# Attention units of a decoder kernel in another order, half adds placed before the next row maximum, samples moved forward, and output weights loaded and split inside the attention loop

## The reference

```python
conv_out = silu(layer_norm(depthwise_causal(a_ext, w_dw) + b_dw))
s = q @ k.T * 64 ** -0.5 + (c_q - c_k)          # c: running sums of log forget gates
att = softmax(where(pos_k <= pos_q, s, -inf)) @ v   # 8 heads of 64
mix = concat([conv_out, att]) @ w_out_even      # 1024 x 1024
```

## Time and profile before

| | us |
|---|---|
| median of 3 runs | 2755.68 (2751.33 to 2757.24) |
| profiled execution, its own time | 2756.72 |
| its span in the profile | 2755.1 |
| TensorE busy | 2581.8 (94%) |
| VectorE busy | 1357.0 (49%) |
| ScalarE busy | 711.6 (26%) |
| POOL busy | 427.2 (16%) |
| first row maximum of attention | at 327.54 |
| last row maximum | at 601.22 |
| first matmul of the output product | at 630.57 |

### The profile page before, as it was taken

The page is one execution under the profiler, slowest core; times in us unless marked ns, Lnnn a source line. Parts: engine busy times, 40 slices in busy tenths (PEclk is TensorE's granted clock), DMA queues, the critical chain, the costliest instruction groups (busy, mean ns, idle before and its releaser), DMA issues.

```text
span 2755.1 us, 38472 instructions
## 1 busy us (share of the span) xinstructions
PE 2581.8 (94%) x15545; PEld 2471.4 (90%) x15545; DVE 1357.0 (49%) x2034; ACT 711.6 (26%) x1218; POOL 427.2 (16%) x423
## 2 busy tenths in 40 slices
PE   7999588877899999999999999999999999999996
PEld 7999455557799999999999999988999999999995
DVE  4788755556753323333334644577433333333355
ACT  4110354444341111111111531225211111111114
POOL 3299233322200000000002200032000000000023
PEclk9999799998999999999999999999999999999998
DMA  7110412122011111111111221121111111111101
GB/s 230 50 31 0 137 57 70 54 86 93 25 52 47 40 38 47 47 46 47 44 34 47 60 91 46 38 101 38 47 47 47 41 37 46 46 39 40 45 16 65
DMA packets 169615, 152.55 MB, mean 55 GB/s; under 512 B 17057, under 2 KB 144337, under 8 KB 169432
## 3 DMA queue, kind: packets, MB, share of 16 engines
q1 hardware_dynamic: 161920, 133.92, 16.0%
q0 software_dynamic: 6208, 15.94, 1.8%
q10 hardware_dynamic: 1320, 0.24, 0.1%
HBM read 131.43 MB, written 18.93 MB: 55 GB/s over the span
## 4 chain that ended last, share of the span: by engine, by line
PE 87%; DVE 8%; issue 2%; ACT 2%; DMA 1%; SPq 0%; DVEq 0%; POOL 0%; ACTq 0%
PE PS L746 26%; PE PS L747 26%; PE PS L748 26%; PE PS L964 2%; DVE ST L1738 2%; PE PS L902 1%; DVE AL L1560 1%; PE PS L754 1%; PE PS L906 1%; PE PS L955 1%; DVE SPR L1666 1%; PE PS L919 1%; DVE RSD L1849 1%; PE PS L942 0%; PE PS L760 0%
## 5 line engine op out<-in xcount | busy, mean ns | idle before, releaser
L746 PE MATMUL PS<-AH,WHI 128*128 128x368 f32 x3360 | 1122.4, 334 | 43.6 <-DVE Y L1912 14.1
L747 PE MATMUL PS<-AL,WHI 128*128 128x368 f32 x3360 | 1114.8, 332 | 0.0
L748 PE MATMUL PS<-AH,WLO 128*128 128x368 f32 x3360 | 1111.3, 331 | 0.0
L746 PEld LDWEIGHTS PS<-AH,WHI 128*128 128x128 f32 x3360 | 635.3, 189 | 54.5 <-DVE Y L1912 18.2
L747 PEld LDWEIGHTS PS<-AL,WHI 128*128 128x128 f32 x3360 | 634.4, 189 | 2.8 <-issue 0.6
L748 PEld LDWEIGHTS PS<-AH,WLO 128*128 128x128 f32 x3360 | 634.7, 189 | 0.0
L1942 DVE TENSOR_TENSOR HF<-S,PS 128x368 f32<-128x368 f32 x132 | 70.9, 537 | 698.1 <-ACT S L1179 698.1
L746 PE MATMUL PS<-HH,WHI 128*128 128x368 f32 x1056 | 349.9, 331 | 3.2 <-DVE Y L1953 3.2
L747 PE MATMUL PS<-HL,WHI 128*128 128x368 f32 x1056 | 349.6, 331 | 0.0
L748 PE MATMUL PS<-HH,WLO 128*128 128x368 f32 x1056 | 349.3, 331 | 0.0
L1953 DVE TENSOR_TENSOR Y<-Y,PS 128x368 f32<-128x368 f32 x480 | 251.6, 536 | 154.9 <-PE PS L748 154.9
(11 more groups left out here) (267 smaller groups left out, 2250.9 us busy)
## 6 DMA issues: line engine op xcount, KB each, us to landing
RAW<-in_w_ffn_gate SPq DMA_DIRECT2D x44, 512.0 KB, 3.8
RAW<-in_w_ffn_up SPq DMA_DIRECT2D x44, 512.0 KB, 5.0
RAW<-in_w_ffn_down SPq DMA_DIRECT2D x44, 512.0 KB, 3.5
RAW<-in_w_in_even SPq DMA_DIRECT2D x20, 512.0 KB, 4.9
Y<-x_spill SPq DMA_DIRECT2D x16, 552.0 KB, 6.0
KR<-in_cache_k SPq DMA_DIRECT2D x32, 256.0 KB, 3.1
RAW<-in_w_in_odd SPq DMA_DIRECT2D x16, 512.0 KB, 4.5
x_spill<-Y POOLq DMA_DIRECT2D x3, 1472.0 KB, 6.5
```

What stands on the lines that cost most here:

```text
L746: pe.matmul(out, wh, xh, start=first, stop=False)
L747: pe.matmul(out, wh, xl, start=False, stop=False)
L748: return pe.matmul(out, wl, xh, start=False, stop=last)
```

## The change

The order in each head becomes 0, 7, 1, 6, 2, 5, 3 and then 4, 8 or 8, 4, with the sample fourth in odd heads (place 3). The key turns move: an even head h has those of its own sequence at places 1 to 4 and the first two of the next sequence at places 7 and 8; the odd head after it has the other two at places 0 and 1. The page loads, the samples' queries and new keys, and the turn back of a sample's result move with them. On VectorE the half add of n-6 comes before the maximum of n. At the end, output weight rows 0 and 1 are loaded as soon as the last sample's values are done; ScalarE splits them, and makes the first mixed rows, inside the last steps of its loop, and VectorE makes their low parts there. On TensorE the turn back of a sample's result waits for the centring (`la_cen`) instead of the copy of the variance, and the convolution's norm for one sample result more. One of the convolution's reciprocals moves from the loop's last steps to behind it.

```diff
-PAR8 = (1, 1, 0, 0, 1, 1, 0, 0)
-HEADS = tuple((0, 1, 2, 3, 4, 5) + ((None,) if h % 2 else ()) + ((6, 8, 7), (6, 7, 8))[PAR8[h]] for h in range(NH))
+HEADS = ((0, 7, 1, 6, 2, 5, 3, 4, 8),
+         (0, 7, 1, None, 6, 2, 5, 3, 4, 8),
+         (0, 7, 1, 6, 2, 5, 3, 8, 4),
+         (0, 7, 1, None, 6, 2, 5, 3, 8, 4),
...
         def key_turn(n):
-            return (h, r - 1) if h < NH and 1 <= r < 5 else None
+            if h == NH:
+                return None
+            if h % 2 == 0:
+                return (h, r - 1) if 1 <= r < 5 else (h + 1, r - 7) if 7 <= r < 9 else None
+            return (h, r + 2) if r < 2 else None
```

In SyncE's queue:

```diff
                 if k == 6:
-                    sp.wait_ge(qk_done, 1 + SMP[-1])
+                    sp.wait_ge(pv_done, 2 + SMP[-1])
+                    for n in (0, 1):
+                        load(2 * ST_OUT0 + n, (2 * ST_OUT0 + n) % 4, out_rows(0, n))
                     sp.wait_ge(sb_done, NS // 2)
                     sp.wait_ge(att_evac, 1 + NU)
-                    for n in range(4):
+                    for n in (2, 3):
                         load(2 * ST_OUT0 + n, (2 * ST_OUT0 + n) % 4, out_rows(0, n))
```

In POOL's loop:

```diff
-                if h % 2 and r == 3:
+                if h % 2 and r == 0:
                     new_keys(h // 2)
```

In ScalarE's loop and behind it:

```diff
+                if n in (NU + 1, NU + 2):
+                    act.wait_ge(pv_done, 2 + SMP[-1])
+                    split_centred(ST_OUT0, (n - NU - 1,))
+                if n == NU + 3:
+                    act.wait_ge(qk_done, NU)
+                    act.wait_ge(att_evac, 1 + FIRST[4])
+                    mix_high(2, QKV, (0, 1))
+                if n == NU + 4:
+                    act.wait_ge(sb_evac, NS // 2)
+                    mix_high(2, QKV, (2,))
...
-                if h % 2 and r == 2 and n < NU:
+                if h % 2 and r == 1 and n < NU:
                     queries(h // 2)
...
-            split_centred(ST_OUT0)
             act.wait_ge(att_evac, 1 + NU)
-            mix_high(2, QKV)
             mix_high(3, QKV)
             split_centred(ST_OUT0 + 1)
```

In VectorE's loop and behind it:

```diff
                     inverse(*UNITS[n - 1])
+                if n > LAG_V:
+                    gathered(*UNITS[n - LAG_V - 1])
                 if n < NU:
                     peak(*UNITS[n])
-                if n > LAG_V:
-                    gathered(*UNITS[n - LAG_V - 1])
...
-                if NU < n <= NU + 2:
-                    inverse_conv(n - NU - 1)
-            split_centred(ST_OUT0)
+                if n == NU + 1:
+                    inverse_conv(0)
+                if n in (NU + 2, NU + 3):
+                    split_centred(ST_OUT0, (n - NU - 2,))
+                if n == NU + 4:
+                    mix_low(2, (0, 1))
+            mix_low(2, (2,))
+            inverse_conv(1)
```

More of the change, by code:

```diff
@@ L374, in build @@
         BACK = {u + LAG_V + 3: p for p, u in enumerate(SMP)}
-        assert all(place(n)[1] == 4 or n >= NU for n in BACK)
+        assert all(place(n)[1] == 1 or n >= NU for n in BACK)
         def norm_step(n, h0, r0):
@@ L478, in _ @@
             for h in range(NH - 1):
[L479 to L482, removed]
+                if h % 2 == 0:
+                    key_pages(h + 1)
+                    if h:
+                        values(h + 1)
+                else:
+                    key_pages(h + 1)
                     values(h + 1)
+                    value_pages(h // 2 + 1)
             def residual(k):
@@ L971, in turn_back @@
                 pe.wait_ge(exp_done, WIDE[2 * p + 1] + 3)
-                if p < NC:
-                    pe.wait_ge(la_copy, p + 1)
+                pe.wait_ge(la_cen, 2 * min(p + 1, NC))
                 for c in range(HT):
@@ L980, in conv_norm @@
                 pe.wait_ge(exp_done, WIDE[h - 1] + 3)
-                pe.wait_ge(sb_evac, (h - 1) // 2)
+                pe.wait_ge(sb_evac, h // 2)
                 norm_product(ONES_H, YSA, s_in, s_res, c, 2)
@@ L1305, in _, with mix_high @@
             act.copy(CQ2[64:128, :], KBS[0:64, PAST:KS]).then_inc(cq_ready, 1)
+            def mix_high(q, src, cs=range(NC)):
+                for c in cs:
+                    act.copy(AH[:, 2 * q:2 * q + 2, chunk(c)], src[:, 2 * q % 4:2 * q % 4 + 2, chunk(c)]).then_inc(la_hi, 1)
             for n in range(NU + LAG_V + 1):
@@ L1336, in _ @@
                     head_high(h + 1, r - 3)
-            split_centred(ST_OUT0)
[L1339 to L1343, removed]
             act.wait_ge(att_evac, 1 + NU)
-            act.wait_ge(sb_evac, NS // 2)
-            mix_high(2, QKV)
             mix_high(3, QKV)
@@ L1793, in inverse_conv, with mix_low @@
                 dve.reciprocal(RSV[:, c, :], RSV[:, c, :]).then_inc(la_rs, 1)
+            def mix_low(q, cs=range(NC)):
+                for c in cs:
+                    src, qs = AEXT if q < 2 else QKV, slice(2 * q, 2 * q + 2)
+                    dve.wait_ge(la_hi, 3 * OUT_TILES[0].index(q) + c + 1)
+                    low(AL[:, qs, chunk(c)], src[:, 2 * q % 4:2 * q % 4 + 2, chunk(c)], AH[:, qs, chunk(c)]).then_inc(m_ready, 1)
             for n in range(NU + LAG_V + 1):
@@ L1815, in _ @@
                     head_low(h + 1, r - 5)
-                if NU < n <= NU + 2:
-                    inverse_conv(n - NU - 1)
-            split_centred(ST_OUT0)
[L1821 to L1826, removed]
+                if n == NU + 1:
[6 more added lines that the diff above has]
+            inverse_conv(1)
             def mix_low_even(o):
-                if o == 0:
-                    mix_low(2)
                 if o == 1:
```

## The result

The changed kernel takes 2771.01 us (median of 5 runs, 2767.24 to 2776.98) beside 2751.33 for the kernel before on the same chip: ratio 1.0066, 95% interval 1.0048 to 1.0084. (A ratio here is estimated from all runs together with its interval, so it differs a little from the quotient of two medians.) It is slower, by 16 us in the profiled execution (own time 2772.58 against 2756.72; span 2770.9 against 2755.1).

What follows compares the result with a forecast made beforehand. It took attention to be bound by VectorE and ScalarE handing each other work while TensorE waits. Loop +7.1, clock +4 and tail -15.25 gave -4.1 us: 2752.6, or 2752 as median, range 2736 to 2770.

Steps and rivals of the forecast that it cites:

- the walk: Attention loop stepped through in each engine's queue order at full clock: 280.8 us against 273.7 before, +7.1 us.
- the key turn's wait for the copy of bank 6: Sign in the attention loop: TensorE's key turns wait above 15 us for ScalarE's copy instead of 6.4, singly 2 to 4.
- the half adds' wait: Sign in the attention loop: TensorE's value products wait well under 35 us for VectorE's half add, 35.3 us before.
- the maximum waiting for ScalarE through the half add: Sign on VectorE: the row maximum no longer waits for scores alone but for ScalarE's half copy, by way of the half add.
- the loads before the last maximum: Sign at the loop's end: loads of the output weights are issued before the last row maximum.
- The tail: From last row maximum to output product: early output weights start the product 14.1 us after it instead of 29.35, -15.25 us.
- the clock term: Attention loop: TensorE's lost clock adds 4 us, half of 9 us, with slow matmuls hidden more often; ends 0 and +9.
- the sum: Whole kernel: +7.1 loop, +4 clock, -15.25 tail make -4.1 us, so 2752.6 us against the profiled execution's 2756.72.
- Rival 2: Attention loop: longer standing at key turns drops the clock at some 12 places, +22 us on the walk, 2770 us; chance 0.20.
- The half adds: VectorE's half add before the maximum: removes up to 35.3 us of TensorE's wait, but queues the maximum behind ScalarE's half copy.
- all 35.3 us go: Lower bound of the loop term: TensorE's whole wait for half adds vanishes and nothing replaces it, -31 us.
- The later steps: From the output product on: steps keep their distances from its start, so they add no time.

Runs made afterwards that it cites:

- kept-busy kernel: Changed kernel plus 8 needless matmuls of 512 columns before the key turns at 12 places: 2758.27 us, ratio 1.0021 to the kernel before.
- the two that free the key turn: Changed kernel with bank 6 copied before the exponential, 2737.38 us, ratio 0.995; changed kernel with key turns behind value products, 2751.63 us, ratio 0.9998.

## Why the prediction was wrong

**What held.** The rows of the walk came as said: the key turn's wait for the copy of bank 6 above 15 us (30.9 in 13, longest 3.3; 3.6 had been walked), the half adds' wait "well under 35" (11.3), the maximum waiting for ScalarE through the half add, the loads before the last maximum. The tail was predicted at 14.1 us and took 14.94.

**The step that failed is the clock term**, "I take half, +4, with 0 and +9 as ends". The walk at full clock gave 280.8 us, the loop took 301.39: 20.6 us beside a term of 4. These 16.6 us are most of the 20 us by which the profiled execution missed the sum; the tail is 0.8 and the later steps 2.5. By heads the excess over the walk is 2.0, 3.9, 2.4, 2.1, 1.5, 4.0, 2.4 and 2.3 us, largest in heads 1 and 5, whose clock is 0.83 and 0.85. The argument had been that slow matmuls would be "hidden more often" since TensorE waits more. It was the wrong way round: in these traces the clock falls in or just behind waits, and the slow matmuls come right behind, in front of the next scores (512.53 to 515.45 above) that all engines wait for. The clock lost is 0.14 x 301 = 42 us against 0.08 x 274 = 22 before. The amount was the fault: I had carried over the 15 us of before, though my walk had just found TensorE standing longer at places 3, 4 and 8.

How much of the 20.6 us is clock is shown only in part. The kept-busy kernel took 3.0 of the 4.0 us of excess from head 5 and 2.7 of 3.9 from head 1 by a higher clock, 6.0 over the loop. The rates at hand, 0.6 us for each us lost before and 2.9 for 3.5 between the two head 2, make 42 us of clock 25 to 35 us by estimate, more than the excess, so the clock could be all of it. But the walk has an error of its own that these runs don't separate: heads 4 and 7, at 0.95, lost 1.6 and 1.9 us of clock and lie 1.5 and 2.3 over it.

**Rival 2 is nearest to what happened**: it named the key turns, about 12 places, the fall of the clock (below 0.88) and 2770 us. The kept-busy kernel and the two that free the key turn bear out its mechanism. That its number came out is partly luck: it had a low stretch behind each key wait, while seven of the 13 started one, and the other four of the eleven stretches stand behind waits for the half add and a DMA. It had a chance of 0.20 and the range ended on its number; the evidence for more was in the walk itself. Its reason against, that the 2.4 us wait at 419.47 cost no clock, was one place: after the change a wait of 2.17 us had a fall (437.04), one of 2.25 us had none (522.93), and one and the same wait of 2.25 us had it in one execution and not in another.

**The half adds.** Pricing them by one walk with the order was right, and the bound that all 35.3 us go was far off. Alone they cost 0.3%, in the changed kernel they do nothing measurable, and with the key turns freed they gain some 0.6%. In the changed order they also took part in the clock's fall, by the three low stretches behind waits for them.

**The later steps.** Said to keep their distances; they took 2.5 us more. In the first 120 us of the output product the granted clock is 0.91 against 0.96 before, with the same busy time (105.2 and 105.8 us) for 548 matmuls instead of 574. Why it is lower there wasn't tried.

## What to carry to other kernels

Where a hand walk finds the matrix engine standing for 2 to 3 us again and again, price a low clock behind those stands too (here a low stretch began in or behind 11 of 17 waits of 1.5 us and more), and not only the stand; an amount of lost clock taken over from the kernel before is no use when the number of stands changes. When work moves to a step where a shared PSUM bank is still full, look at what stands in front of the copy that empties it: here one copy, moved ahead of an exponential into idle time of its engine, turned 0.7% slower into 0.5% faster. Test an edit of one queue's order together with the order of the others, since the half add in front cost 0.3%, did nothing or gained 0.6% by what stood around it.

## What the runs showed of the hardware

- Ninety-six needless matmuls of 512 columns made the kernel faster: mean granted clock of the loop 0.92 instead of 0.86, loop 295.4 instead of 301.4 us, ratio 1.0021 instead of 1.0066.
- The length of a wait doesn't decide by itself. After 2.90 us without a matmul the clock stood at 0.50 for 5.5 us; after 2.25 us, ten us later, it stayed at 1.00. A wait of 2.17 us had a fall (437.04), and the same wait of 2.25 us, in two executions of one kernel, was followed by 8 us at 1.00 in one and at 0.57 in the other.
- The same kernel measured 1.0066 and later 1.0115, with intervals apart. In the two profiles head 2, same instructions, took 35.60 us at a clock of 0.86 and 38.51 at 0.78: 3.5 us of clock more lost and 2.9 us more length.
